# Output projection of an encoder layer on one core: a 2x2 block product with seven products in place of the plain one

## The reference

```python
hproj = x @ w_in[l]
...
mixed = g_na * (y_na @ w_branch_na[l]) + g_ml * (y_ml @ w_branch_ml[l])
x = layer_norm(DEEPNORM_ALPHA * x + mixed @ w_out[l], ln1_g[l], ln1_b[l])
f = conv_glu(x, ffn_w_up[l], ffn_conv_w[l], ffn_conv_b[l], ffn_w_down[l])
x = layer_norm(DEEPNORM_ALPHA * x + f, ln2_g[l], ln2_b[l])
```

## Time and profile before

| | |
|---|---|
| median of three runs | 2829.03 us |
| the profiled execution: its own time | 2834.71 us |
| its span, first to last instruction | 2833.0 us |
| busy in the span: PE, DVE, ACT | 97%, 62%, 43% |
| matmuls | 16059 |
| mean granted TensorE clock | 0.987 of full speed |
| output projection on TensorE, by the trace | from 1296.9 us to 1471.2 us |
| moved by DMA over the span | 140 GB/s in the mean |

### The profile page before, as it was taken

The page is one execution under the profiler, slowest core; times in us unless marked ns, Lnnn a source line. Parts: engine busy times, 40 slices in busy tenths (PEclk is TensorE's granted clock), DMA queues, the critical chain, the costliest instruction groups (busy, mean ns, idle before and its releaser), DMA issues.

```text
span 2833.0 us, 42473 instructions
## 1 busy us (share of the span) xinstructions
PE 2761.5 (97%) x16059; PEld 2438.2 (86%) x16059; DVE 1751.2 (62%) x2404; ACT 1221.5 (43%) x1837; POOL 210.2 (7%) x272
## 2 busy tenths in 40 slices
PE   8999999999999999999988999999999999999995
PEld 7788888888888888888878999999999999888884
DVE  4465454555433333334357888888888876778788
ACT  4344444443332222223236555555555554444444
POOL 2000001110000000000010111111111101000000
PEclk9999999999999999999998999999999999999998
DMA  4333333333333333333335677777777768357452
GB/s 152 93 87 86 88 92 91 82 89 77 83 90 97 96 96 96 96 96 126 127 118 134 163 203 198 194 175 202 192 192 175 197 179 317 142 214 257 151 187 88
DMA packets 469489, 397.97 MB, mean 140 GB/s; under 512 B 16360, under 2 KB 418076, under 8 KB 466144
## 3 DMA queue, kind: packets, MB, share of 16 engines
q1 hardware_dynamic: 401440, 302.04, 35.1%
q0 software_dynamic: 65120, 89.68, 13.2%
q10 hardware_dynamic: 2784, 4.26, 0.4%
HBM read 346.60 MB, written 49.33 MB: 140 GB/s over the span
## 4 chain that ended last, share of the span: by engine, by line
PE 89%; DVE 7%; DMA 2%; issue 1%; ACT 1%; ACTq 0%; DVEq 0%
PE ps L1707 16%; PE ps L1709 16%; PE ps L1708 16%; PE ps L1978 13%; PE ps L1980 13%; PE ps L1979 13%; PE ps L1701 1%; DVE uw L1378 1%; PE ps L1917 1%; DMA racc<-h_dram 1%; ACT uw L863 1%; DVE aop L1449 1%; DMA hx<-hn_dram 0%; PE ps L1897 0%; DMA x_tok<-in_x 0%
## 5 line engine op out<-in xcount | busy, mean ns | idle before, releaser
L1034 DVE TENSOR_TENSOR wlo<-raw,whi 128x512 fp32r<-128x512 f32 x480 | 330.7, 692 | 755.0 <-ACT whi L624 753.4
L1978 PE MATMUL ps<-aop,uw 128*128 128x256 f32 x2408 | 685.1, 285 | 9.4 <-DVE aop L1449 5.6
L1979 PE MATMUL ps<-aop,uw 128*128 128x256 f32 x2408 | 683.1, 284 | 0.0
L1980 PE MATMUL ps<-aop,uw 128*128 128x256 f32 x2408 | 683.0, 284 | 0.0
L624 ACT ACTIVATE whi<-raw 128x512 fp32r<-128x512 f32 x480 | 300.9, 630 | 864.4 <-PE ps L1709 863.8
L1707 PE MATMUL ps<-xt_hi,whi 128*128 128x512 f32 x1408 | 554.4, 394 | 1.7 <-DVE wlo L1034 1.7
L1709 PE MATMUL ps<-xt_hi,wlo 128*128 128x512 f32 x1408 | 549.8, 390 | 0.0
L1708 PE MATMUL ps<-xt_lo,whi 128*128 128x512 f32 x1408 | 549.6, 390 | 0.0
L1978 PEld LDWEIGHTS ps<-aop,uw 128*128 128x128 f32 x2408 | 463.9, 193 | 13.2 <-DVE aop L1449 6.3
L1979 PEld LDWEIGHTS ps<-aop,uw 128*128 128x128 f32 x2408 | 464.0, 193 | 0.0
L1980 PEld LDWEIGHTS ps<-aop,uw 128*128 128x128 f32 x2408 | 464.0, 193 | 0.0
(11 more groups left out here) (267 smaller groups left out, 3275.1 us busy)
## 6 DMA issues: line engine op xcount, KB each, us to landing
raw<-in_w_in SPq DMA_DIRECT2D x352, 256.0 KB, 2.7
quad<-in_ffn_w_up SPq DMA_DIRECT2D x172, 512.0 KB, 4.0
region<-in_ffn_w_down SPq DMA_DIRECT2D x32, 1280.0 KB, 9.7
a_dram<-ah SPq DMA_DIRECT2D x20, 1792.0 KB, 9.5
aopb<-a_dram POOLq DMA_DIRECT2D x28, 1280.0 KB, 8.5
quad<-in_ffn_w_up POOLq DMA_DIRECT2D x43, 512.0 KB, 7.2
raw<-in_w_out SPq DMA_DIRECT2D x64, 256.0 KB, 3.0
raw<-in_w_branch_ml SPq DMA_DIRECT2D x32, 256.0 KB, 2.6
```

The lines of the kernel that those rows point to most:

```text
L1034: nc.vector.tensor_tensor(wlo[:, k % HL, :], raw[:, k % RAW, :], whi[:, k % HL, :].bitcast(F32), ALU.subtract).then_inc(w_lo_ready, 1)
L1978: mm(o, a_hi, b_hi, start=first, stop=False, skip_group_check=True)
L1979: mm(o, a_hi, b_lo, start=False, stop=False, skip_group_check=True)
L1980: return mm(o, a_lo, b_hi, start=False, stop=last, skip_group_check=True)
```

## The change

The tokens are cut into two halves of 256, the 16 blocks of the inner dimension into even and odd ones (a pair of blocks per merge iteration), and the output columns of a step into two groups of 512. Such a 2x2 by 2x2 block product needs eight block products, and in the scheme used here (the Winograd form of Strassen's) it takes seven, with sums formed of the operands before and of the results after.

- **During the merge** the two halves of an iteration write into one tile `mb` (slots 7 and 2, then 0 and 1). DVE forms the four sums of the activations in slots 3 to 6 (`pair_sums`, three instructions), ACT and DVE split all seven operands into `mh` (`pair_hi`, `pair_lo`, 128x1792), and POOL stores them in `m_dram` (1792 KB a pair, eight pairs). The last iteration runs all gate units first, then all branch units; its second half is mixed and its pair split only after the output projection has begun.
- **The output projection** has four steps: two groups of four pairs (the inner dimension), each by two halves of the columns. A step has seven products of two pieces. A piece is two pairs by two token tiles by three, 12 matmuls of 128x512. The stationary operands `opw` come from `m_dram` by POOL (1024 KB each; step 2 needs new ones), the four quadrants of `w_out` by SP (1024 KB each). ACT and DVE split 14 pieces a step, and DVE forms eight half sums of weights (`w_form`).
- **Results** are added into `res` as in the down projection: seven adds of 128x1024 a step on DVE, and three copies on ACT (`seed_w`, `p5_w`, `u2_w`). `x` is loaded in eight tiles of 512 KB.
- The statistics of the norm are taken within the last step and behind it. On DVE the first weight operands of the up projection and `form(0, 1)` now stand ahead of the last add.
- Counters and one buffer (`hs`, third slot) are moved; the stages behind are otherwise as they were.

The diff, cut to its core:

```diff
-        mixed = sb("mixed", [P, KB, S], 160 * K)
+        mb = sb("mb", [P, 8, 256], 160 * K)
+        mh = [sb(f"mh{n}", [P, 7, 2, 256], at * K, F32R) for n, at in enumerate((168, 136))]
...
+        opw = [sb(f"opw{n}", [P, W_PAIRS, 2, 256], at * K, F32R) for n, at in enumerate(W_OP_AT)]
+        w_region = [sb(f"w_region{n}", [P, W_PAIRS, 512], at * K) for n, at in enumerate(W_REGION_AT)]
...
+            for p in range(W_PAIRS * W_GROUPS - 1):
+                spill_pair(p)
+            pool.wait_ge(s["m_out"], 16 * W_PAIRS)
+            pool.wait_ge(unit_used, U_LAST + 16 + HL)
+            for o in OPS[:4]:
+                w_op(0, o)
+            pool.wait_ge(unit_used, U_END + HL)
+            pool.wait_ge(s["mix_done"], KB + 1)
+            w_op(0, OPS[4])
+            x_piece(0, 0)
+            x_piece(1, 0)
+            w_op(0, OPS[5])
+            x_piece(0, 1)
+            x_piece(1, 1)
+            w_op(0, OPS[6])
+            spill_pair(W_PAIRS * W_GROUPS - 1)
+            for n in (2, 3):
+                for h in range(2):
+                    x_piece(h, n)
+            pool.wait_ge(s["m_out"], 16 * W_PAIRS * W_GROUPS)
+            for i, o in enumerate(OPS):
+                pool.wait_ge(s["op_used"], w_piece(1, i, 1) + 1)
+                w_op(1, o)
...
+            for step in range(W_STEPS):
+                for i in range(7):
+                    for pc in range(2):
+                        if pc == 0:
+                            if i == 5:
+                                c11_w(step)
+                            elif i == 6:
+                                c22_w(step)
+                            elif i == 0 and step:
+                                c12_w(step - 1)
+                            elif i == 1 and step:
+                                c21_w(step - 1)
+                        elif i == 4:
+                            p5_w(step)
+                        elif i == 5:
+                            u2_w(step)
+                        operand_lo(w_piece(step, i, pc))
+                        if i in (0, 1, 3, 5):
+                            w_form(step, (0, 1, 3, 5).index(i), pc)
+                        if step == 0 and pc == 1 and i == 0:
+                            dve.wait_ge(unit_used, U_END + HL)
+                            dve.wait_ge(s["merge_sg"], KB + 1)
+                            dve.wait_ge(s["mix_done"], KB)
+                            mix(1, 6, mg[1])
+                            pair_sums(KB // 2 - 1)
+                        if step == 0 and pc == 1 and i == 2:
+                            pair_lo(KB // 2 - 1)
...
+            c12_w(last)
+            operand_lo(N_W)
+            w_stats(0, 3, s["c12_done"], W_STEPS)
+            operand_lo(N_W + 1)
+            form(0, 1)
+            c21_w(last)
+            w_stats(1, 2, s["c21_done"], W_STEPS)
...
-            for i in range(2):
-                for half in range(2):
-                    pe.wait_ge(s["wo_free"], i * 2 + half + 1)
-                    for k in range(KB):
-                        pe.wait_ge(s["mxlo_done"], k + 1)
-                        one_by_four(i * 32 + U_WO, 16 * half + k, k, KB, 4 - 4 * half, mx_hi, mx_lo,
-                                    s["wo_tiles"] if half and k == KB - 1 else None)
+            for step in range(W_STEPS):
+                for i in range(7):
+                    o, bank = OPS[i], PRODUCT_BANK[i]
+                    for pc in range(2):
+                        n = w_piece(step, i, pc)
+                        pe.wait_ge(s["op_lo"], n + 1)
+                        if pc == 0:
+                            pe.wait_ge(a_op_in[o], 16 * (step // 2 + 1))
...
+                        for kk in range(2):
+                            k = 2 * pc + kk
+                            for t in range(2):
+                                ts = slice(t * P, (t + 1) * P)
+                                last = add_three(ps[:, bank + t, :], opw[o][:, k, 0, ts], opw[o][:, k, 1, ts],
+                                                 dw[:, n % 3, 0, kk, :], dw[:, n % 3, 1, kk, :], i < 2 and k == 0, k == W_PAIRS - 1)
+                        last.then_inc(s["op_used"], 1)
```

More of the change, by code:

```diff
@@ L87, with regions @@
 RES_AT = ((44, 90, 24, 58), (74, 138, 28, 164))
-def regions():
-    held, spare, out = (2, 3, 0, 1), 4, []
-    for step in range(N_STEPS):
+def regions(held, spare, steps):
+    out = []
+    for step in range(steps):
         out.append(held)
@@ L97, in regions, with w_uses, w_piece @@
     return out
-REGIONS = regions()
+REGIONS = regions((2, 3, 0, 1), 4, N_STEPS)
+W_REGIONS = regions((0, 1, 2, 3), 4, W_STEPS)
+def w_uses(step, r):
+    return sum(r in held for held in W_REGIONS[:step + 1])
+def w_piece(step, i, pc):
+    return 14 * step + 2 * i + pc
 def piece(step, i, pc):
@@ L304, in build @@
         quad_in = [[sem(f"quad_in{n}{q}") for q in range(4)] for n in range(2)]
+        w_quad_in = [sem(f"w_quad_in{n}") for n in range(5)]
         t1_in = [sem(f"t1_in{n}") for n in range(2)]
@@ L572, in _ @@
             add_b11(1)
[L573 removed]
+            pool.wait_ge(s["a_lo_done"], 16)
             load_chunk(0)
@@ new lines, in first_add, with c11_w @@
+            def first_add(r, term, op, done):
+                nc.vector.scalar_tensor_tensor(r, r, ALPHA, term, ALU.mult, op).then_inc(done, 1)
+            def c11_w(step):
+                dve.wait_ge(s["op_used"], w_piece(step, 3, 1) + 1)
+                r = res_tile(0, 2 * (step % 2))
+                if step < 2:
+                    dve.wait_ge(res_piece_in[2 * step], 32)
+                    first_add(r, pair(0), ALU.add, s["c11_done"])
+                else:
+                    nc.vector.tensor_tensor(r, r, pair(0), ALU.add).then_inc(s["c11_done"], 1)
@@ new lines, in c21_w, with w_stats @@
+            def c21_w(step):
+                dve.wait_ge(s["op_used"], w_piece(step, 6, 1) + 1)
+                r = res_tile(1, 2 * (step % 2))
+                if step < 2:
+                    dve.wait_ge(res_piece_in[2 * step], 32)
+                    first_add(r, pair(2), ALU.add, s["c21_done"])
+                else:
+                    nc.vector.tensor_tensor(r, r, pair(2), ALU.add).then_inc(s["c21_done"], 1)
+            def w_stats(h, n, done, count):
+                dve.wait_ge(done, count)
+                for t in range(2 * h, 2 * h + 2):
+                    ins = nc.vector.bn_stats(st[:, t, n, :], res[:, t, n * 512:(n + 1) * 512])
+                link(ins)
@@ new lines, in _, with add_three @@
+            for half in range(2):
+                if half == 0:
+                    pe.wait_ge(s["mix_done"], KB - 1)
+                for k in range(4):
+                    y_hi, y_lo = ((yml_hi, yml_lo), (yna_hi, yna_lo))[k // 2]
+                    four_by_one(U_LAST, 16 + 4 * half + k, k % 2, 8, ps[:, 2 + 4 * half + k // 2, :], y_hi, y_lo)
+            def add_three(o, a_hi, a_lo, b_hi, b_lo, first, last):
+                mm(o, a_hi, b_hi, start=first, stop=False, skip_group_check=True)
+                mm(o, a_hi, b_lo, start=False, stop=False, skip_group_check=True)
+                return mm(o, a_lo, b_hi, start=False, stop=last, skip_group_check=True)
```

549 lines of the change are left out of this document (348 added, 201 removed).

## The result

| | before | after |
|---|---|---|
| median, four runs each, same chip | 2829.02 us (2827.96 to 2832.36) | 2814.00 us (2811.58 to 2819.01) |
| the profiled execution: its own time | 2834.71 us | 2812.55 us |
| its span | 2833.0 us | 2810.5 us |
| matmuls | 16059 | 15963 |
| first matmul of the output projection to the first of the up projection | 200.6 us | 182.1 us |

The ratio is 0.9945, with a 95% interval from 0.9933 to 0.9957: 15.0 us less, the interval from 12.2 to 19.0. The prediction was 18.4 less than the median, 2810.6; the measured median is 3.4 above it and inside its range. By this median alone it can't be told from rival B (2815.1) or C (2812.7), and it lies above the 2808.5 to 2812.6 that the prediction gave its own forecast A; what tells them apart is the trace. The stage that the change touches became 18.5 us shorter there, beside 18.4 forecast.

A forecast was written before the change was run, and what follows sets the result against it. It took TensorE's matmul issue to bound the output projection. Profiled execution: 2834.71 - 21.7 (matmuls) + 3.3 (tail) = 2816.3 us; against the median, 2829.03 - 18.4 = 2810.6 us, range 2806.5 to 2819.

The forecast's parts named there:

- rival B: Output projection's start stumbles on late tiles as the down projection's did, about 4.5 us: 2815.1 us; chance 0.20.
- rival C: DVE instructions cost their full duration, 1.22 us in place of 1.135: 2812.7 us; chance 0.10.
- forecast A: The prediction's own case for the whole kernel: 18.4 us less, 2810.6 us, own range 2808.5 to 2812.6; chance 0.50.
- Matmuls, 21.7 us: Output projection: 672 matmuls in place of 768, same shape and pace, 96 x 0.2265 = 21.7 us less.
- rival F: Output projection: new stationary tiles or short pieces slow the matmul pace, no gain, 3.3 us lost: 2832 us; chance 0.03.
- Merge at no cost: Merge: the added sums and splits on DVE and ACT cost 0; without cover 1.7 to 3.6 us an iteration.
- The start: Step 0: third piece ready at U + 4.8 (U: output projection's start), wanted at U + 5.44; no wait.
- POOL's list: Step 0: queued x tiles and operands land at about U + 15 to 17, fourth tile's deadline U + 22.2.
- Rival E: POOL's queue serves one transfer at a time, fourth x tile at U + 43.5, 35 us lost: 2846 us; chance 0.05.
- Steps 1 and 2: Output projection: DVE 29 x 1.135 = 32.9 us of 38.05 a step, ACT 17.9; no wait.
- The tail, 3.3 us: Last step: DVE never waits from S + 13.0 (S: step 3's start), aggregate at S + 45.0; 3.3 us given back.
- Rival D: Last step: DVE gains slack earlier, so the tail costs 1 us instead of 3.3: 2808.3 us; chance 0.08.

The follow-up runs named there:

- Experiment 7: Changed kernel with the third and fourth tile of x queued on POOL behind step 0's last operand and the last pair's store: 2814.85 us, ratio 0.9947.
- Experiments 5: Changed kernel with four extra DVE additions of 128x1024 in each of steps 1 and 2: 2813.27 us, ratio 0.9944.
- experiment 6: Changed kernel with eight extra DVE additions of 128x1024 in each of steps 1 and 2: 2818.16 us, ratio 0.9958.
- Experiment 4: Changed kernel with each bn_stats of the first norm reading 16 columns in place of 512: 2808.3 us, ratio 0.9923.
- experiment 2: Changed kernel with two groups of statistics moved into step 2 and one behind product 2 of step 3: 2810.03 us, ratio 0.9928.
- experiment 3: Experiment 2 plus `form(0, 1)` and its loads moved into step 2 (one up projection operand then differs): 2810.74 us, ratio 0.9929.
- 8: Experiment 2 with `form(0, 1)` done by GpSimd, after VectorE's split of the same quadrant: 2809.86 us, ratio 0.9927.

## Why the prediction was right, point by point

- *Matmuls, 21.7 us.* Shown. 672 on `opw`, steps of 38.0 us with 169 matmuls in a window, no slower pace; rival F is out.
- *Merge at no cost.* From 900 to 1290 us PE is busy for all of 390 us, with 1722 matmuls in both traces, while DVE works 143.85 us instead of 123.61.
- *The start.* Third piece at U + 4.9 for U + 4.8, no wait of PE in step 0. What is 0.6 us wide here was reckoned from durations of the kernel before and met to 0.1.
- *POOL's list.* All x tiles are there in time. Rival E (2846 us) would have the fourth at U + 43.5; it was there by U + 17. One count in the argument for this rival was wrong: 24 of DVE's 28 instructions a step read two operands from SBUF (14 splits, 8 sums, 2 of the 6 adds), and not 20 of 29. The transfers came in time beside them. Experiment 7 shows that the wait it feared is real once the tiles are late, and has the place and the deadline that the prediction named.
- *Steps 1 and 2.* No wait of PE, as forecast. The list was one add too long: 28 instructions make 31.8 us at their distance of starts, not 32.9, and this cost nothing, as there was room either way. Experiments 5 and 6 put the edge between 32 and 36 instructions a step. By 1.135 us it lies at 33.5 (38.05/1.135), by 1.22 at 31.2; rival C is out.
- *The tail, 3.3 us.* The aggregate stands at S + 45.0 to the tenth, and its two parts are met as well: the last wait ends at S + 13.1 for 13.0, and from there it takes 31.9 us for 32.0. Experiment 4 shows that statistics make most of DVE's lateness. Rival D (DVE has caught up) is out: the up projection starts 18.5 us earlier and not 20.7.
- *The argument on the tail that was too simple* came in the expectations, not in the prediction: for experiments 2 and 3 I took what is moved out of step 3 at its full price. It is worth that in full only if it leaves the stretch in which DVE never waits. In experiment 2 this stretch starts at 1426.91, 18.8 us into the step, and 2.6 expected became 1.5; in 3 and 8 the sum left it and gave 1.1 of 1.1 beyond experiment 2.
- *The stumbling start, rival B.* Nothing of it at the start of the stage. In the down projection, where the pattern came from, it still stumbles. The windows there, which answer to the earlier trace rows:

```profile
2380.00:2385.00 5.00, 4.44 (x20) 3.68 (x21) 3.81 (x4) 0.00 (x0) 0.00 (x0) 1.00 1.04 417
2385.00:2390.00 5.00, 5.00 (x24) 4.14 (x23) 2.36 (x2) 1.06 (x1) 0.00 (x0) 1.00 1.03 413
...
2395.00:2400.00 5.00, 4.48 (x20) 3.44 (x19) 5.00 (x6) 0.63 (x1) 0.00 (x0) 1.00 0.55 211
```

PE loses 0.56 + 0.52 us, with 2.4 us of DVE's waiting for `racc` (2.8 before), but the clock stays at full speed, where the earlier trace rows had 0.77 and 0.89. From its first matmul on `x_hi` to the first on `aopb` that stretch took 37.5 us before and 35.5 after, on the same instructions.

So the profiled executions differ by 18.5 us in the stage, 1.6 ahead of it (it starts at 1295.3 instead of 1296.9), 2.0 in that stretch and 0.4 elsewhere: 22.5 us of span. Nothing shows that more than the first belongs to the change. The 1.6 us are made between 90 and 110 us, where the granted clock was 0.76 and 0.90 before and 0.85 and 0.98 after, 10 x 0.09 + 10 x 0.08 = 1.7 us; and the stretch of 35.5 us lasts between 34.5 and 37.3 in the nine traces of the changed kernel and its variants. The medians give 15.0 and 18.8 us; 18.5 lies inside both intervals (to 19.0 and to 20.1). That the single median came out 3.4 us off the forecast is within what such a comparison can tell.

## What to carry to other kernels

Where TensorE is full, a block product with seven products is worth its matmuls times their pace, less what VectorE's extra work leaves behind at the end of the stage; list VectorE's instructions from the point from which it no longer waits, at their distance of starts. Here the end came out to 0.1 us; where the point had moved and the list was not made anew (experiment 2) it was off by 1.1. An instruction moved out of a stage's end gives back its price only if it leaves that unbroken stretch, and an engine with nothing to do (GpSimd here) can take one whose result is wanted late. When a change of 18 us is to be read from single executions, compare the distance between two points inside the stage rather than the totals.

## What was not expected of the hardware

The granted clock differs between profiled executions at places where the code is the same, and this makes most of the difference in when they reach the output projection. Two windows near the start of the program, first in experiment 3, then in experiment 4 (full speed is 2.4 GHz, the lower level 1.2 GHz):

```profile
90.00:100.00 10.00, 9.24 (x60) 7.73 (x61) 5.04 (x9) 3.99 (x6) 0.52 (x1) 0.78 0.46 133
100.00:110.00 10.00, 10.00 (x41) 8.18 (x40) 2.34 (x6) 2.81 (x4) 0.59 (x1) 0.88 0.34 105
```

```profile
90.00:100.00 10.00, 9.44 (x70) 7.90 (x69) 4.93 (x10) 3.91 (x5) 0.52 (x1) 1.00 0.49 133
100.00:110.00 10.00, 10.00 (x45) 8.27 (x45) 2.41 (x7) 3.22 (x5) 0.59 (x1) 1.00 0.48 137
```

Experiment 3 reached the output projection at 1297.3 us, experiment 4 at 1293.5, with 3.4 us of difference made in the clock of these two windows (10 x 0.22 + 10 x 0.12). Over the nine traces that have the changed kernel's stages ahead of it the start lies between 1293.5 and 1297.3. In the three where both windows read 1.00 it is 1293.5 to 1294.0; in the five where they lack 1.7 us, 1294.0 to 1295.3. It is so at the up projection as well: experiments 2 and 8 begin it at the same time (1474.57 and 1474.56), and in the window from 1475 to 1480 the clock is 0.71 in one and 0.91 in the other. The gap of 1.37 us in the last step of the changed kernel left the clock at 1.00 until the last matmul, as did the six gaps of up to 1.1 us in the middle steps of experiment 6. What decides in which execution the clock is lower at the same place stays open.
